# Two transformer blocks on one core: the spatial tiles of the mixer's output interleaved with the scans of its recurrent unit

## What is computed

```python
y_gm = _spatial_gating(gelu(z_gm), v_g, v_b, ws, bs)          # u * (mask(ws) @ layernorm(v) + bs)
xr = _causal_dwconv(x_lru, lru_conv_w, lru_conv_b)
r, i = sigmoid(xr @ wa + ba), sigmoid(xr @ wx + bx)           # per head of 128
log_a = -8.0 * r * softplus(-lam)
a, mult = exp(log_a), sqrt(-expm1(2.0 * log_a))
h[t] = a[t] * h[t - 1] + mult[t] * i[t] * xr[t]               # the scan
y_lru = h * gelu(g_lru)
y = concatenate([rmsnorm(y_gm, gm_out_g), rmsnorm(y_lru, lru_out_g)])
x = x + y @ w_out
```

## Time and profile before

| | us |
|---|---|
| median of 3 runs | 2385.78 |
| lowest and highest run | 2379.47, 2387.15 |
| the profiled execution | 2380.07 |
| its span in the profile | 2378.3 |
| TensorE busy | 2286.2 |
| VectorE busy | 1311.4 |
| ScalarE busy | 1043.1 |
| GpSimd busy | 266.3 |

### The profile page before, as it was taken

The page is one execution under the profiler, slowest core; times in us unless marked ns, Lnnn a source line. Parts: engine busy times, 40 slices in busy tenths (PEclk is TensorE's granted clock), DMA queues, the critical chain, the costliest instruction groups (busy, mean ns, idle before and its releaser), DMA issues.

```text
span 2378.3 us, 30943 instructions
## 1 busy us (share of the span) xinstructions
PE 2286.2 (96%) x12255; PEld 1857.3 (78%) x12255; DVE 1311.4 (55%) x2114; ACT 1043.1 (44%) x1606; POOL 266.3 (11%) x333
## 2 busy tenths in 40 slices
PE   5889999999999999999999998999999999999998
PEld 2457777777777866778888886888888888888887
DVE  2443533332323264545676767667765777567764
ACT  2222333332322155445554465456544555355543
POOL 1000000000001022100010424111100110001111
PEclk9889999999999999999999999999999999999999
DMA  9764433345655465734566544555555565565552
GB/s 367 275 244 176 142 123 133 127 136 168 221 183 177 160 236 182 260 106 146 185 192 214 176 142 156 172 186 187 187 194 186 187 195 187 192 188 187 190 189 81
DMA packets 346895, 436.16 MB, mean 183 GB/s; under 512 B 13848, under 2 KB 269280, under 8 KB 345856
## 3 DMA queue, kind: packets, MB, share of 16 engines
q1 hardware_dynamic: 341376, 413.19, 52.5%
q0 software_dynamic: 3280, 15.86, 1.8%
q10 hardware_dynamic: 2096, 5.15, 0.6%
HBM read 427.85 MB, written 6.29 MB: 183 GB/s over the span
## 4 chain that ended last, share of the span: by engine, by line
PE 87%; DVE 5%; ACT 3%; DMA 3%; issue 1%; POOL 1%; SPq 0%; ACTq 0%; POOLq 0%
PE ps L1287 30%; PE ps L1288 16%; PE ps L1262 5%; PE ps L1264 5%; PE ps L1263 5%; PE ps L1282 5%; PE ps L1284 5%; PE ps L1283 5%; PE ps L1243 3%; DVE SPL L1726 2%; ACT SPL L1491 2%; DMA RAW<-in_w_in_dram 1%; PE ps L1336 1%; PE ps L1353 1%; DMA RAW<-in_ada_w_dram 1%
## 5 line engine op out<-in xcount | busy, mean ns | idle before, releaser
L1287 PE MATMUL ps<-HS,SPL 128*128 128x512 f32 x3456 | 1215.8, 396 | 14.5 <-DVE SPL L1726 9.6
L1726 DVE TENSOR_TENSOR SPL<-RAW,SPL 128x1024 fp32r<-128x1024 f32 x592 | 751.6, 1273 | 603.2 <-ACT SPL L1491 600.5
L1288 PE MATMUL ps<-HS,SPL 128*128 128x256 f32 x3456 | 968.4, 280 | 0.0
L1491 ACT ACTIVATE SPL<-RAW 128x1024 fp32r<-128x1024 f32 x592 | 621.7, 1055 | 475.1 <-PE ps L1288 281.3
L1287 PEld LDWEIGHTS ps<-HS,SPL 128*128 128x128 f32 x3456 | 649.5, 188 | 167.4 <-DVE SPL L1726 8.4
L1288 PEld LDWEIGHTS ps<-HS,SPL 128*128 128x128 f32 x3456 | 654.4, 189 | 1.9 <-issue 1.7
L1262 PE MATMUL ps<-SPL,HS 128*128 128x512 f32 x576 | 250.5, 435 | 21.1 <-ACT XT L1533 6.7
L1264 PE MATMUL ps<-SPL,HS 128*128 128x512 f32 x576 | 230.8, 401 | 0.0
L1263 PE MATMUL ps<-SPL,HS 128*128 128x512 f32 x576 | 230.8, 401 | 0.0
L1282 PE MATMUL ps<-HS,SPL 128*128 128x512 f32 x480 | 195.4, 407 | 1.2 <-DVE HS L1882 1.2
L1284 PE MATMUL ps<-HS,SPL 128*128 128x512 f32 x480 | 187.7, 391 | 0.0
(11 more groups left out here) (272 smaller groups left out, 1701.3 us busy)
## 6 DMA issues: line engine op xcount, KB each, us to landing
RAW<-in_w_in_dram SPq DMA_DIRECT2D x208, 512.0 KB, 5.8
RAW<-in_ada_w_dram SPq DMA_DIRECT2D x192, 512.0 KB, 4.9
RAW<-in_ffn_w_up_dram SPq DMA_DIRECT2D x192, 512.0 KB, 3.6
RAW<-in_w_out_dram SPq DMA_DIRECT2D x96, 512.0 KB, 4.4
RAW<-in_ffn_w_down_dram SPq DMA_DIRECT2D x96, 512.0 KB, 3.3
x_spill<-XT POOLq DMA_DIRECT2D x2, 2048.0 KB, 15.4
XT<-x_spill POOLq DMA_DIRECT2D x1, 4096.0 KB, 17.4
MM<-in_x_dram ACTq DMA_DIRECT2D x2, 1024.0 KB, 10.8
```

Source lines behind the costliest of these rows:

```text
L1287: mm(PS[b][:, :], wr, hh, start=k == 0, stop=False, skip_group_check=True)
L1288: m = mm(PS[b][:, 256:512], wl, hh[:, 0:256], start=False, stop=k == KT - 1, skip_group_check=True)
L1491: act(SPL[:, (n - 1) % NSPL, 0, :], raw_of(i), ACT.Copy).then_inc(s_hi, 1)
L1726: tt(w[:, 1, :], raw_of(s["i"]), w[:, 0, :].bitcast(F32), ALU.subtract).then_inc(s_lo, 1)
```

## The change

All scans followed by calls of `ready_gm` become pairs: scan j, then the whole tile j (`y0`, `y1`, `y2` put one behind the other, not staggered). `ready_gm(k)` then only names the tile's semaphore.

```diff
-        ready_gm = on_demand([split_tile("gm", k, UU[:, k, :], V(c_gmo + k), RSG, HH[1][:, k, :, :], lambda: [y["gm_rs"]], done_gm) for k in range(8)], done_gm)
+        tiles_gm = [split_tile("gm", k, UU[:, k, :], V(c_gmo + k), RSG, HH[1][:, k, :, :], lambda: [y["gm_rs"]], done_gm) for k in range(8)]
+        ready_gm = lambda k: [done_gm[k]]
...
         run_chunks(marks[7])
-        hi.extend([lru_exp(j) for j in range(8)] + [lambda j=j: put("lru_scan", j=j) for j in range(8)]
-                  + [lambda k=k: ready_gm(k) for k in range(8)])
+        def tile_gm(k):
+            return lambda: flush(list(tiles_gm[k]))
+
+        hi.extend([lru_exp(j) for j in range(8)] + [step for j in range(8) for step in (lambda j=j: put("lru_scan", j=j), tile_gm(j))])
         run_chunks(marks[8])
```

## The result

| us | before | changed |
|---|---|---|
| median of 10 runs each | 2381.67 | 2390.73 |
| lowest and highest | 2376.22, 2387.15 | 2385.98, 2396.24 |
| span of the profiled execution | 2378.3 | 2386.2 |
| its own time | 2380.07 | 2388.0 |

The ratio of the changed kernel's time to that of before is 1.0035, with a 95% interval of 1.0021 to 1.005: 8.3 us slower, 5.0 to 11.9 by the interval. The forecast of +6.2 us lies inside, and whether that is more than 0.3% is as undecided as the chances had it.

The account below looks back on a forecast made before the run. Until 1468 the in-order queues of ScalarE, VectorE and GpSimd bound the stage, elsewhere TensorE. Trips 18.8, splits 8.2 and contention 1.6 make 28.6 us against 22.1, less 0.2: +6.2 on the median 2385.78, forecast 2392.0, range 2382 to 2400.

Parts of the forecast that it names:

- The round trip: Between the table loads, ScalarE and VectorE wait for each other per scan and tile: 2.35 us, eight times, 18.8.
- Splits and join inside trips: Weight splits and the column join standing among the eight scan-and-tile trips on VectorE and ScalarE add 8.2 us.
- Contention: GpSimd's low part delays VectorE's next multiply by 0.3 us behind trips 1, 2, 4, 5 and 7; 1.6 with roundings.
- The sum: First square root to second table load takes 28.6 us, before 22.1; less 0.2 for the old order's walk, +6.2.
- TensorE's waits to grow from 9.6 to about 15: In the stage of scans and tiles, TensorE's idle time before matmuls waiting for VectorE's splits (L1726) grows this much.
- The rival of half clock: TensorE at 1.2 GHz behind 1460 becomes the bound: at worst +6.3 us on top, 2398.3; chance 0.12.
- the 1.7 us of slack: TensorE's spare time before the next stage's start, taken off the cost of half-clock chunks behind 1460.
- More loss in the trips: Rival: multiplies lose 0.55 us five times and each of eight trips 0.1 more: +8.2, 2394; chance 0.12.
- free trips: Rival: round trips cost nothing because VectorE always finds other work; table load near 1446, -2 us, 2383.8; chance 0.08.
- splits all in time: Rival: evenly spread tiles let each split come in time and TensorE's 9.6 us of waits go: 2376; chance 0.03.

Follow-up runs that it names:

- e6_low_late: Changed kernel, but GpSimd's low part of tile j waits until scan j+1 is through; ratio to before 1.003 (1.0018 to 1.0041).
- e2_staggered: Changed kernel, but the tiles between the scans are staggered: scale of tile j, high part of j-1, low part of j-2; ratio to before 0.9991.
- e8_before_again: The kernel before, unaltered, run once more for a second profile; ratio to before 0.9999 (0.9987 to 1.0012).
- e7_changed_again: The changed kernel, unaltered, run once more for a second profile; ratio to before 1.0023 (1.0009 to 1.0037).
- e1: Changed kernel, but all eight square roots are put ahead of the first scan; ratio to before 1.0007 (0.9986 to 1.0027).
- e3: Changed kernel with half the change undone: all eight scans first, then eight whole, unstaggered tiles; ratio to before 1.0013 (0.9996 to 1.003).
- e4: Changed kernel, but the whole tiles move to empty entries of the stage before, two per group; ratio to before 1.0016 (0.9999 to 1.0033).
- e5: Tiles in the stage before, two per group, but staggered over the four empty entries instead of whole; ratio to before 0.9992 (0.9978 to 1.0007).
- e9_early_staggered_again: The kernel with staggered tiles in the stage before, unaltered, run once more; ratio to before 0.9991 (0.9981 to 1.0001).

## Why the prediction was right

- **The round trip, 2.35 a trip, 18.8 in all.** In trip 1 of the changed kernel the legs are 1425.86, 1426.31, 1426.77, 1427.38, 1427.87 and 1428.19, so 2.33. Right, and shown by what is cut: without the leg over the square root I falls by 4.1, with the scale an entry ahead by 5.9.
- **Splits and join inside trips, 8.2.** The split comes between scan and scale in trips 2, 5 and 8 (1430.02 is the first) and behind the high part on ScalarE in 3 and 6; VectorE's wait of 1.43 in trip 6 is in the rows above. Right in place, and about right in size: the eight trips take 28.33 - 8 x 2.33 = 9.7 us more than eight bare ones, and less the 1.75 of contention that leaves 7.9.
- **Contention, five multiplies by 0.3.** Five it is, behind trips 1, 2, 4, 5 and 7, with 0.35 each, 1.75 in all against 1.6. The run that moves GpSimd away gave 1.53 back. The Trainium skill (SBUF — State Buffer, "Who interferes with whom") says that a VectorE instruction with two inputs in SBUF contends with a GpSimd instruction that reads SBUF, and one with at most one such input does not. The traces agree: the multiply (two operands in SBUF) is held, and the scale (second factor from PSUM) is not, but that second half rests on the kernel before, 0.47 at 1444.20; in the changed kernel no scale runs beside GpSimd.
- **The sum, 28.6 against 22.1.** Measured 28.33 against 22.08, so +6.25 for +6.2 forecast. The closeness is in part luck: the walk of the new order came out 0.3 too long, and the 0.2 taken off for the old one made that nearly good. That the next stage's start follows the table load: +6.1 at 1474.32.
- **TensorE's waits to grow from 9.6 to about 15.** Wrong: 11.3. The figure takes a chunk at 3.1 us throughout and leaves the half-clock chunks out. Four stretches at 1.2 GHz filled the gaps: the matmuls of L1290 take 470 ns at the mean in place of 432. The waits shrank and the starts stayed where the splits put them. The end was not touched, and the step was not part of the sum.
- **The rival of half clock.** It was right in its premise (more such stretches: near 1431, 1438, 1448 and 1462) and wrong in its conclusion, by a small margin. Up to 1460.17 TensorE came later than a split only once: the one that ended at 1453.33 was taken up near 1453.85, and the wait of 2.94 behind it swallows that half microsecond. From 1460.17 on TensorE works for 13.9 us without a wait and takes up the next three chunks (near 1464.3, 1467.5 and 1470.3) each 0.3 to 1.4 us after its split. The stretch near 1462 lies in there, and of the 1.7 us of slack in the prediction 0.26 is left, the wait before 1474.32. A second stretch behind 1460 would have moved the end, as the rival says; in e6_low_late two in a row did, by 0.7 us.
- **More loss in the trips, free trips, splits all in time.** The repeats at 28.33 and 28.34 leave no room for any of the three.
- **The size of the whole.** 8.3 by the first comparison, 5.5 by the second (0.0023 x 2382.59). The stage explains 6.1 to 6.2, which both intervals hold. The remainder of either is scatter by the finding below, not a further mechanism that I can show.

## What to carry to other kernels

A step that crosses between in-order engines should have other work between its halves on both of them. Scale, high part and low part cost their instructions when staggered by an entry, and the latency of every crossing when put whole; where the tiles stood mattered less than that (4.25 us for the form alone; for the place alone 0.35 with staggered tiles and 2.0 with whole ones, 28.33 against 26.33). And when two chains share two engines in turn, look for the one instruction that couples them, here a square root with its input long ready, standing behind a high part that waited; moving it up took 4.1 us off the stretch. Judge such an edit by intervals inside the stage, which repeat to 0.01 us between the two profiles of a kernel, before asking the whole time, which scatters by 10.

## What the runs showed that I had not expected

**TensorE has two paces at one granted clock.** Outside the waits, in the long stages behind this one, it is busy all the time and PEclk is 1.00. Yet the same kernel does not do the same number of matmuls there. Before, and before once more, 2050 to 2250:

```profile
2050.00:2250.00 200.00, 200.00 (x1157) 176.34 (x1156) 136.94 (x194) 106.39 (x152) 17.05 (x28) 1.00 0.60 190
```

```profile
2050.00:2250.00 200.00, 200.00 (x1134) 173.46 (x1133) 134.71 (x189) 104.38 (x149) 16.09 (x26) 1.00 0.61 187
```

That is 172.9 and 176.4 us per thousand matmuls. Taken over 600 matmuls from the n-th on, by their starts, the pace is one of two numbers (ns per matmul):

| profile | n = 7700 | n = 9400 | n = 10600 |
|---|---|---|---|
| before; e2_staggered | 173.3 | 173.3 | 173.3 |
| e8_before_again; changed; e6_low_late | 173.3 | 173.3 | 176.7 |
| e7_changed_again | 176.7 | 173.3 | 173.3 |
| e1, e3, e4, e5 | 176.7 | 176.7 | 173.3 |
| e9_early_staggered_again | 176.7 | 173.3 | 176.7 |

In these blocks nothing lies between, and the level goes with the execution, not with the kernel: before shows both in the last column. In all eleven profiles it changes only near the same four places, the 7650th, 8700th, 10250th and 11750th matmul. The step is 1.9%; over 1200 matmuls it makes 4 us, half of the whole effect studied here. From the 7145th matmul to the end the profiles take 905.7 to 913.8 us, and the two in which all three blocks of the table are fast take 905.7 and 906.2, the others 908.1 or more; so the pace makes most of the scatter behind the stage. It is not all of the scatter: the 6300th matmul starts between 1302.7 and 1309.1 us, and a spread of 6.0 us stands there already at the 700th. DMA share and the other engines' work hardly differ between the two rows above. The cause of the two paces stays open.

**Half clock can be free, or not.** In the stage four stretches at 1.2 GHz cost the changed kernel nothing in the end: three lay ahead of waits, and the fourth used up slack, of which 0.26 us was left. The single stretch at 1485 in the first profile of before lay where TensorE was the limit and cost 1.6 us.

**A scan is held too.** At 1433.03 the scan with both inputs in SBUF took 1.11 us in place of 0.69 while GpSimd was at the join.
